# A two-block transformer kernel: modulation moved to VectorE, and norms, ring loads, splits and stores put elsewhere in the program

## The chip, the cores and the metric

The kernel runs on one core of one Trainium2 chip. The metric is the device time of one execution in microseconds (us). Before the change the median of three runs is 3538.93 us, from 3534.08 to 3541.27.

The engines are TensorE (PE, matmuls and weight loads), VectorE (DVE), ScalarE (ACT), GpSimd (POOL) and SyncE (SP, here only a queue that issues DMAs). Each executes its own program in order, and they wait for each other through semaphores.

## What is computed

One sequence of 512 tokens of width 1024 in float32 goes through two blocks.

```python
def first_block(x, ...):
    h = rmsnorm(x, norm_mix_g)
    gq, gk, gv, gr, glr, sq, sk, sv, gate_a, gate_b = split(h @ w_in)
    y_a = gla(gq, gk, gv, log_sigmoid(glr @ w_gk2 + b_gk)) -> rmsnorm * silu(gr) @ w_branch_a
    y_b = sliding window attention(rope(rmsnorm(sq)), rope(rmsnorm(sk)), sv, sinks) @ w_branch_b
    x = x + (sigmoid(gate_a) * y_a + sigmoid(gate_b) * y_b) @ w_out
    return x + peer_layer(rmsnorm(x, norm_ffn_g), ...)

def second_block(x, c, ...):
    shift1, scale1, gate1, shift2, scale2, gate2 = split(silu(c) @ w_ada + b_ada)   # modulation
    h = rms_norm(x, g_mix) * (1 + scale1) + shift1
    q_a, lat, k_r, iq, ik, iw, q_b, k_b, v_b, f_b = split(h @ w_in)
    o_a = attention over the 256 (at most) keys that an indexer (iq, ik, iw) picks, on a latent of rank 128
    o_b = forgetting attention(q_b, k_b, v_b, f_b)
    x = x + gate1 * (concat(rms_norm(o_a, g_out_a), rms_norm(o_b, g_out_b)) @ w_out)
    h2 = rms_norm(x, g_ffn) * (1 + scale2) + shift2
    return rms_norm(x + gate2 * peer_ffn(h2, ...), g_final)
```

`w_ada` is 1024 x 6144, so the modulation is one vector of 1024 times a matrix of 24 MB. A PEER layer scores 128 keys twice for 8 heads, picks 16 of 16,384 experts for each token and head, and computes `sum(gate * gelu(x . u[expert]) * v[expert])`.

## The kernel before, in words

**Precision and ring.** Every product is made of three matmuls in `float32r` (`three`): high by high, high by low, low by high. The weights come in units of 1 MB (128 x 2048). SP loads unit m into a ring of R = 2 slots (L259), ACT rounds it to its high part (`split_hi`, L268), DVE subtracts to get the low part (`split_lo`, L276), and only then may PE use the unit (`unit` waits for it) and SP load unit m + 2 into the slot. The program of each engine is written as a list of calls in the order of the stages; that order alone says what stands ahead of what.

**Stages**, with their times in the profiled execution: the first norm and GLA (0 to 235 us); sliding projections, six units sqkv (235.5 to 349); sliding attention, four blocks n of 128 queries in groups g, with the units ga and wa of branch a between them (349 to 523); the join with units gb, wb, wo (523 to 658); the norm and scores of the first PEER layer (to 773); its up stage, 64 units of `peer_u` in two halves each (to 1402); its down stage, 64 units of `peer_v` (1404 to 1936); the second norm, mixers' projections m2 and qa, keys, dots and qkvb (1936 to 2105); attention turns i = 0 to 17 of the mixers (to 2238); mixed norm and wo2 (to 2320); the second PEER layer, the same way (up from 2320, down from 3006, final norm to 3540).

**Modulation.** SP loads `w_ada` in 30 steps s (10 in the GLA stage, 20 in the sliding stages) into rows of `xres` that are free; POOL multiplies by silu(c) (L548), halves the row twice (L551), and sums into 128 columns (L556, event `ada_sum`); PE sums over partitions with matmuls of one column (L566, `ada_pe`); DVE adds the bias (L577). Some instructions of other stages wait for `ada_sum` too, since they reuse its memory.

**Sliding unit on DVE.** For each unit: sum of squares over a head (L1057), mean and reciprocal (L360, L362), scaling (L1062, L1064), rotation (L350 to L356), a copy to the layout for transposes (L1071), then the split of the unit after next, and the copies of its projection from PSUM (L339).

**PEER.** `peer_order` is a planner that yields `up`, `spread`, `dot` and pick steps in one order, which each engine's program walks. In the spread DVE builds one-hot products (L1791, L1796) that PE multiplies into dense gates; ACT copies them (L1591), SP stores them (`store`, L1419) to `gbuf`; each up unit's gelu is stored to `hbuf` (`keep`, L1411). In the down stage SP fetches both back (`fetch`), DVE and ACT make weighed products Wp (high, low, `weigh_act`, L1852), and PE multiplies them with `peer_v` (L1525). DVE also gathers back single rows (L1758, L1775), loaded by POOL (L1888). At u = 9 of the first down stage DVE makes the second block's row `g_mix * (1 + scale1)` (`modulated_dve`, L1240).

**Mixed norm.** `mixed_act`, `mixed_dve`, `mixed_pe` square all four blocks, take the roots, scale (L2462), transpose all blocks, and only then start wo2.

## Time and profile before

| what | value |
|---|---|
| median of three runs | 3538.93 us (3534.08 to 3541.27) |
| profiled execution, its own time | 3541.71 us |
| its span, first to last instruction | 3539.9 us |
| mean granted clock of TensorE | 0.972 of full speed |
| PE busy | 3338.2 us, 94% |
| DVE busy | 2672.7 us, 76% |
| ACT busy | 1400.4 us, 40% |
| POOL busy | 1031.9 us, 29% |
| DMA, mean over the span | 242 GB/s |

The busy share says that PE has work nearly always; it does not say which wait ends last in a stage. In the timeline each row has the start and length in us, the engine, the line of the kernel and the operation, then what it writes and reads, and in brackets how long the engine was idle before it and which engine's work ended that. A clock of 1.00 is 2.4 GHz and 0.50 is 1.2 GHz; a window that holds both levels has a value between.

### The profile page before, as it was taken

The page shows a single profiled execution, that of the slowest core. Times are in us where ns is not written, and L with a number is a line of the kernel's source. Part 1 is how long each engine was busy: PE and PEld are TensorE (multiplying, and loading weights), DVE is VectorE, ACT ScalarE, POOL GpSimd, SP SyncE. Part 2 cuts the span into 40 slices and gives each one's busy share as a digit, 9 for nine tenths or more (in the row PEclk, how much of TensorE's full clock was granted, in tenths as well). Part 3 has the DMA queues.
Part 4 walks back from the last instruction along what each step waited for, and adds up shares of the span by engine and source line. Part 5 has one row for each costly group of instructions (what it writes and reads, how often), then busy time and mean ns, then how long its engine had stood idle before and what let it go on. Part 6 is the DMA issues. An engine that isn't in the chain of part 4 may idle for free. (4 is left out here: it accounts for less than half of the span.)

```text
span 3539.9 us, 46446 instructions
## 1 busy us (share of the span) xinstructions
PE 3338.2 (94%) x18703; PEld 2946.8 (83%) x18703; DVE 2672.7 (76%) x4561; ACT 1400.4 (40%) x1899; POOL 1031.9 (29%) x652
## 2 busy tenths in 40 slices
PE   8997899999999998999999899889999999999998
PEld 7967558889999898788887786789999898888887
DVE  4458654349999895788888497549999896788888
ACT  4322452233333574233333345333333575333333
POOL 6516700002444330333332000002443331333332
PEclk9998999999999999999999899899999999999999
DMA  6313313237898899899997120226888899999996
GB/s 227 108 51 140 109 54 119 90 99 263 301 326 306 297 345 326 321 359 360 363 360 276 54 72 7 84 73 240 313 314 311 290 349 326 350 362 359 360 361 248
DMA packets 330506, 855.56 MB, mean 242 GB/s; under 512 B 22258, under 2 KB 188066, under 8 KB 297139
## 3 DMA queue, kind: packets, MB, share of 16 engines
q1 hardware_dynamic: 256562, 584.12, 47.1%
q0 software_dynamic: 73728, 268.47, 20.7%
q8 instruction: 147, 2.41, 0.3%
q14 instruction: 69, 0.56, 0.0%
HBM read 746.58 MB, written 105.93 MB: 241 GB/s over the span
## 5 line engine op out<-in xcount | busy, mean ns | idle before, releaser
L293 PE MATMUL ps<-ht_hi,parts 128*128 128x384 f32 (+2 forms) x5088 | 1373.8, 348 | 38.5 <-DVE parts L276 38.1
L276 DVE TENSOR_TENSOR parts<-ring,parts 128x2048 fp32r<-128x2048 f32 (+1 forms) x317 | 741.9, 2340 | 357.0 <-ACT parts L268 356.7
L293 PEld LDWEIGHTS ps<-ht_hi,parts 128*128 128x128 f32 x5088 | 936.6, 191 | 85.7 <-DVE parts L276 48.9
L268 ACT ACTIVATE parts<-ring 128x2048 fp32r<-128x2048 f32 (+1 forms) x317 | 606.7, 1914 | 831.7 <-PE ps L1525 677.2
L293 PE MATMUL ps<-ht_lo,parts 128*128 128x384 f32 (+2 forms) x2544 | 877.5, 345 | 0.0
L1888 POOL DMA_INDIRECT scr<-in_p_rows_u,cst x256 | 403.3, 1575 | 885.9 <-DVE scr L1758 563.9
L335 ACT ACTIVATE scr<-ps 128x384 f32<-128x384 f32 (+2 forms) x497 | 244.4, 505 | 942.0 <-PE ps L293 879.6
L1888 POOL DMA_INDIRECT scr<-in_peer_v,cst x256 | 375.3, 1466 | 770.2 <-DVE xres L1775 620.3
L1525 PE MATMUL ps<-parts,ht_lo 128*128 128x512 f32 x2304 | 530.2, 390 | 6.5 <-DVE ht_lo L1852 6.5
L1525 PE MATMUL ps<-parts,ht_hi 128*128 128x512 f32 x2304 | 529.3, 390 | 4.5 <-DVE ht_hi L1852 4.5
L1525 PEld LDWEIGHTS ps<-parts,ht_lo 128*128 128x128 f32 x2304 | 434.4, 189 | 97.3 <-DVE ht_lo L1852 6.9
L1525 PEld LDWEIGHTS ps<-parts,ht_hi 128*128 128x128 f32 x2304 | 433.5, 188 | 95.3 <-DVE ht_hi L1852 5.1
L293 PEld LDWEIGHTS ps<-ht_lo,parts 128*128 128x128 f32 x2544 | 485.7, 191 | 16.1 <-issue 0.2
L293 PE MATMUL ps<-parts,ht_hi 128*128 128x256 f32 (+1 forms) x1792 | 340.1, 292 | 27.8 <-DVE parts L276 19.9
L1775 DVE SCALAR_TENSOR_TENSOR xres<-scr,cst,xres 128x1024 f32<-128x1024 f32 x255 | 327.5, 1284 | 27.4 <-DVE xres L1775 0.5
L293 PEld LDWEIGHTS ps<-parts,ht_hi 128*128 128x128 f32 x1792 | 292.0, 200 | 29.8 <-DVE parts L276 20.2
L1758 DVE SCALAR_TENSOR_TENSOR scr<-scr,xres 128x1024 f32<-128x1024 f32 x256 | 306.8, 1218 | 4.2 <-DMA scr<-in_p_rows_u,cst 4.0
L293 PE MATMUL ps<-scr 128*128 128x128 f16 (+7 forms) x2272 | 246.6, 272 | 31.6 <-DVE scr L1796 23.2
L293 PE MATMUL ps<-parts,ht_lo 128*128 128x256 f32 (+1 forms) x896 | 260.4, 291 | 0.0
L293 PEld LDWEIGHTS ps<-scr 128*128 128x128 f16 (+3 forms) x2272 | 187.4, 131 | 85.0 <-issue 32.0
L1591 ACT ACTIVATE scr<-ps 128x512 f32<-128x512 f32 x192 | 195.3, 1159 | 24.7 <-PE ps L293 19.7
L339 DVE COPY scr<-ps 128x256 f32<-128x256 f32 (+2 forms) x74 | 37.0, 519 | 196.1 <-PE ps L293 159.1
(255 smaller groups left out, 2787.4 us busy)
## 6 DMA issues: line engine op xcount, KB each, us to landing
ring<-in_peer_u SPq DMA_DIRECT2D x128, 1024.0 KB, 6.8
ring<-in_peer_v SPq DMA_DIRECT2D x128, 1024.0 KB, 7.5
hbuf<-scr SPq DMA_DIRECT2D x128, 384.0 KB, 7.0
gbuf<-scr SPq DMA_DIRECT2D x96, 512.0 KB, 8.6
scr<-gbuf SPq DMA_DIRECT2D x64, 768.0 KB, 9.3
scr<-hbuf SPq DMA_DIRECT2D x64, 768.0 KB, 11.9
ring<-in_w_in SPq DMA_DIRECT2D x35, 1024.0 KB, 5.4
xres<-in_w_ada SPq DMA_DIRECT2D x18, 1024.0 KB, 7.4
```

The costliest lines, as they stand in the source:

```text
L268: e.activation(halves(m)[0], slot_view(m)[:, 0:units[m][0]], ACT.Copy).then_inc(A.sem, A.up(("hi", m)))
L276: e.tensor_tensor(lo, slot_view(m)[:, 0:units[m][0]], hi.bitcast(F32), ALU.subtract).then_inc(V.sem, V.up(("lo", m), ("slot", m)))
L293: ins = e.matmul(ps, l, r, start=(i == 0), stop=(i == n - 1))
L335: e.activation(dst, src, func).then_inc(A.sem, A.up(("free", key), *names))
L339: e.tensor_copy(dst, src).then_inc(V.sem, V.up(("free", key), *names))
L1525: ins = e.matmul(PSt[:, b * 512:(b + 1) * 512], l, r, start=(u == 0 and k == 0), stop=(u == NU - 1 and k == 5), skip_group_check=True)
L1591: e.activation(self.GS[u % 2][:, :, t0:t0 + 4].rearrange("p i t -> p t i"), psum(key).rearrange("p (t i) -> p t i", t=4), ACT.Copy, scale= ...
L1758: e.scalar_tensor_tensor(out=ur, in0=ur, scalar=1.0, in1=X[:, 0, :], op0=ALU.mult, op1=ALU.mult, accum_out=self.HD[:, k:k + 1]).then_inc(V ...
L1775: ins = e.scalar_tensor_tensor(out=x0, in0=vr, scalar=wk, in1=x0, op0=ALU.mult, op1=ALU.add)
L1888: e.indirect_dma_start(rows[k % len(rows)], None, table, bass.IndirectOffsetOnAxis(ap=self.EID[:, k:k + 1], axis=0)).then_inc(s.sem, s.up( ...
```

## The change

- **Modulation.** The POOL programs `ada_pool` and `sliding_pool` are gone. SP loads `w_ada` in 48 steps of 512 KB (128 rows of the contraction by 1024 columns; the host sends it in that layout), 24 in the GLA stage and 24 in the join. DVE multiplies each by its column of silu(c) and adds it to an accumulator of 1024 columns, behind the split of the next unit (`ADA_GLA`, `ADA_JOIN`). PE sums over partitions in 6 groups of 8 matmuls. Nothing of it stands in the sliding stages, and the waits for `ada_sum` there are gone. The split of the unit gr 0 moves between the exponentials; Abs, Exp and Ln of the gate move into gk 0; silu's input c is loaded ahead of the first unit.
- **PEER order.** Two up halves come ahead of spread 0. The last two spread steps come behind the dots, each behind one more up half. A unit's ring load goes ahead of the store of the unit before (`keep`) in the pick phase, and in the tail ahead of the last stores of the gates. The first fetch goes from u = 61 to u = 62. The weighed products of unit 0 have a place of their own (`Wp0`) and don't wait for the last up unit.
- **Second block's row**: `modulated_dve` at u = 20 instead of 9.
- **Mixers.** Positions are the first row loaded; the unit splits stand ahead of the angles; rotation of the index queries and of the keys, and the norm of the latent, stand beside the unit qa; the transposes of qa come behind the dots of block n = 1.
- **Mixed norm** by blocks 3, 2, 1, 0: squares in turns i = 11, 13, 15, 17, and the first wo2 unit takes each block as it is ready.

```diff
+        ADA_GLA = {("gq", 0): (0, 3), ("gq", 1): (3, 6), ("gk", 0): (6, 8), ("gk", 1): (8, 12),
+                   ("gv", 0): (12, 15), ("gv", 1): (15, 18), ("gv", 2): (18, 21), ("gv", 3): (21, 24)}
+        ADA_JOIN = {("gb", 0): (24, 26), ("gb", 1): (26, 30), ("gb", 2): (30, 32), ("gb", 3): (32, 36),
+                    ("wb", 0): (36, 37), ("wb", 1): (37, 38), ("wb", 2): (38, 39), ("wb", 3): (39, 40),
+                    ("wo", 0): (40, 43), ("wo", 1): (43, 46), ("wo", 2): (46, 48)}
...
-        def ada_pool(e, w, s):
-            x = ada_in(s).rearrange("p (h n) -> p h n", n=1024)
-            h = len(ada_cols(s))
-            w.wait_ge(*at_point("c_act"))
-            w.wait_ge(*at_point("ada", s))
-            v = x.rearrange("p h (c n) -> p h c n", c=NC)
-            e.tensor_tensor(v, v, bc(ct.unsqueeze(1).unsqueeze(3), [128, h, NC, 128]), ALU.mult).then_inc(G.sem, G.up())
-            for n in (512, 256):
-                w.wait_ge(*G.now())
...
+            if s >= 24:
+                w.wait_ge(*at_point("pv_pe", NB - 1))
+            if s % 24 >= 4:
+                w.wait_ge(*at_point("ada_used", s - 4))
+            e.dma_start(ada_in(s), inp["w_ada_2"][s]).then_inc(dm_mw[s % 4].sem, dm_mw[s % 4].up(("ada", s), by=16))
...
+        def ada_loads(e, w, span):
+
+            for s in range(span[0] + 4, span[1] + 4):
+                if s // 24 == span[0] // 24:
+                    ada_load(e, w, s)
+
+        def ada_dve(e, w, span):
+            for s in range(*span):
+                cc = s % NC
+                acc = ada_acc(s)
+                w.wait_ge(*at_point("c_act"))
+                w.wait_ge(*at_point("ada", s))
+                if cc == 0:
+                    if s % 24:
+                        ada_sums(e, w, s // NC - 1)
+                    ins = e.tensor_scalar(acc, ada_in(s), ct[:, 0:1], None, ALU.mult)
+                else:
+                    w.wait_ge(*V.now())
+                    ins = e.scalar_tensor_tensor(out=acc, in0=ada_in(s), scalar=ct[:, cc:cc + 1], in1=acc, op0=ALU.mult,
+                                                 op1=ALU.add)
+                ins.then_inc(V.sem, V.up(("ada_used", s)))
...
+        def ada_pe(e, w, k):
+            ps = bank(w, ("mods", k))
+            w.wait_ge(*at_point("ada_used", 8 * k + 7))
+            for j in range(8):
+                ins = e.matmul(ps[:, j:j + 1], ada_acc(8 * k)[:, 128 * j:128 * j + 128], one, start=True, stop=True)
+            ins.then_inc(P.sem, P.up(("ps", ("mods", k))))
...
                     cols_major(e, w, (name, s, 0), v, 0)
+                    if (name, s) == ("gk", 1):
+                        ada_pe(e, w, 0)
                     cols_major(e, w, (name, s, 1), v, 128, ("used", m))
...
-                                                   V.sem, V.up(("free", ("la", blk)), ("la", blk)))
             for s in range(4):
                 split_lo(e, w, U["gv", s] + 1)
+                ada_dve(e, w, ADA_GLA["gv", s])
...
+            split_lo(e, w, U["gr", 0] + 1)
...
@@ -920,7 +900,6 @@
             if part == 2:
                 split_lo(e, w, U["wa", s] + 1)
             if part >= 2:
-                w.wait_ge(*at_point("ada_sum", ADA - 1 if s >= 2 else ADA_HALF - 1))
...
+            for _ in range(2):
+                owed -= pace
+                yield "up", at_u // 2, at_u % 2, False
+                at_u += 1
             for i in range(STEPS):
                 yield "spread", i, 0, 0
                 yield from due(one_step, True)
-            yield "spread", STEPS, 0, 0
-            yield "spread", STEPS + 1, 0, 0
             while slot < SLOTS:
                 yield "dot", slot, 0, 0
                 slot += 1
+            for i in range(2):
+                yield "up", at_u // 2, at_u % 2, False
+                at_u += 1
+                yield "spread", STEPS + i, 0, 0
...
+                self.Wp0 = parts_at(2048, 4 * ND).rearrange("p (s j t) -> p s j t", s=2, j=2)
...
+            def W(self, u):
+
+                return self.Wp[u % 4] if u else self.Wp0
...
                 for kind, a, b, _ in order:
                     if kind == "up":
+                        if a not in late and b == 0:
+                            load(e, w, U[tag + "u", a] + R + 1)
                         if b == 0 and a:
                             self.keep(e, w, a - 1)
-                        if b == (1 if a in late else 0):
+                        if a in late and b == 1:
                             load(e, w, U[tag + "u", a] + R + 1)
-                        if (a, b) == (NU - 3, 0):
+                        if (a, b) == (NU - 2, 0):
                             self.fetch(e, w, 0)
                     if kind == "spread" and a >= 4 and a % 4 < 2:
...
             def weigh_act(self, e, w, u):
                 g = u // 2
-                w.wait_ge(*(self.pt("down", u - 4) if u >= 4 else at_point("used", U[self.tag + "u", NU - 1])))
+                if u:
...
-                    if u == 9 and self.nq == 16:
+                    if u == 20 and self.nq == 16:
                         modulated_dve(e, w, "n2", 4096, 6144)
 
...
+            sp_small(e, "positions", POS, inp["positions_2"])
+            sp_row(e, "latent_gain", gkv, row("g_kv_2"))
             sp_row(e, "forget_bias", fb, row("b_forget_2"))
-            sp_row(e, "latent_gain", gkv, row("g_kv_2"))
-            sp_small(e, "positions", POS, inp["positions_2"])
...
-                transposes(e, w, ("iqt", blk), [M2[:, blk, 144 + j * 128:144 + (j + 1) * 128] for j in range(2)])
+                if (name, s) == ("qa", 0):
+                    w.wait_ge(*at_point("iq_turned"))
+                    for blk in range(NB):
+                        transposes(e, w, ("iqt", blk), [M2[:, blk, 144 + j * 128:144 + (j + 1) * 128] for j in range(2)])
+                    w.wait_ge(*at_point("latent"))
...
+                if n == 1:
+                    w.wait_ge(*at_point("qa_turned"))
+                    for blk in range(NB):
+                        transposes(e, w, ("qat", blk), [QA[:, blk, j * 128:(j + 1) * 128] for j in range(4)])
             for s in range(4):
...
+                    w.wait_ge(*at_point("angles"))
+                    e.activation(SIN, RR.rearrange("p (b j) -> p b j", b=NB), ACT.Sin)
+                    e.activation(COS, RC.rearrange("p (b j) -> p b j", b=NB), ACT.Sin).then_inc(A.sem, A.up(("cos2",)))
+                if (name, s) == ("qa", 0):
+                    latent_squares(e, w)
...
                     ins.then_inc(A.sem, A.up(("exp2", i)))
+                if i in (11, 13, 15, 17):
+                    mixed_squares(e, w, 3 - (i - 11) // 2)
+                if i == 16:
+                    for blk in (3, 2, 1):
+                        mixed_root(e, w, blk)
...
+
+        def mixers_dve(e, w):
+            for (name, s), n, dst in m2_parts:
+                split_lo(e, w, U[name, s] + 1)
+                if (name, s) == ("qa", 0):
+                    turned_keys(e, w)
+                for blk in (1, 3):
+                    put_dve(e, w, (name, s, blk), dst[:, blk, :], psum((name, s, blk))[:, 0:n], (name, "dve"))
+                if (name, s) == ("m2", 0):
+                    angles_dve(e, w)
+                if (name, s) == ("qa", 0):
+                    for blk in (1, 3):
+                        put_dve(e, w, ("iqt", blk), IQT[:, :, blk * 128:(blk + 1) * 128],
+                                psum(("iqt", blk))[:, 0:256].rearrange("p (k t) -> p k t", k=2), ("iqt", 1))
...
+        def mixed_turn(e, w, blk):
+            w.wait_ge(*at_point("mix_normed", blk))
+            for j0 in (0, 4):
+                transposes(e, w, ("mt", blk, j0), [MIX[:, blk, j * 128:(j + 1) * 128] for j in range(j0, j0 + 4)])
+
...
-                for j0 in (0, 4):
-                    transposes(e, w, ("mt", blk, j0), [MIX[:, blk, j * 128:(j + 1) * 128] for j in range(j0, j0 + 4)])
-            w.wait_ge(*at_point("ht", "mix"))
-            for s in range(4):
+            for blk in (3, 2, 1):
+                mixed_turn(e, w, blk)
+            m = U["wo2", 0]
+            v = unit(w, m)
+            for blk in (3, 2, 1, 0):
+                w.wait_ge(*at_point("ht", "mix", blk))
+                rows_major(e, w, ("wo2", 0, blk), v, 256, blk, *([("used", m)] if blk == 0 else []))
+                if blk == 3:
+                    mixed_turn(e, w, 0)
+            for s in (1, 2, 3):
                 m = U["wo2", s]
...
-                    e.scalar_tensor_tensor(out=mv, in0=mv, scalar=ssm[:, 2 * blk + s:2 * blk + s + 1],
-                                           in1=go[:, 512 * s:512 * s + 512], op0=ALU.mult, op1=ALU.mult).then_inc(
-                                               V.sem, V.up(("mix_normed", blk)))
-                if blk:
-                    mixed_low(e, w, blk - 1)
-            mixed_low(e, w, NB - 1)
+            for blk in (3, 2, 1):
+                mixed_mean(e, w, blk)
+            for blk in (3, 2, 1):
+                mixed_row(e, w, blk)
+            mixed_low(e, w, 3)
+            mixed_mean(e, w, 0)
+            mixed_row(e, w, 0)
+            for blk in (2, 1, 0):
+                mixed_low(e, w, blk)
```

Three places show how instructions move.

The first is VectorE's order in the GLA stage, from the split made while unit gk 1 is in use on to the first units gv. Before:

```order
L276 TENSOR_TENSOR parts<-ring,parts 128x2048
L339 COPY scr<-ps 128x512
L276 TENSOR_TENSOR parts<-ring,parts 128x2048
L339 COPY scr<-ps 128x256 x2
L276 TENSOR_TENSOR parts<-ring,parts 128x2048
L339 COPY scr<-ps 128x256 x2
```

Now:

```order
L276 TENSOR_TENSOR parts<-ring,parts 128x2048
L557 TENSOR_TENSOR mod_t<-ps,mod_t 128x8
L545 TENSOR_SCALAR scr<-xres,scr 128x1024
L548 SCALAR_TENSOR_TENSOR scr<-xres,scr 128x1024 x3
L339 COPY scr<-ps 128x512
L276 TENSOR_TENSOR parts<-ring,parts 128x2048
L548 SCALAR_TENSOR_TENSOR scr<-xres,scr 128x1024 x3
L339 COPY scr<-ps 128x256 x2
L276 TENSOR_TENSOR parts<-ring,parts 128x2048
L548 SCALAR_TENSOR_TENSOR scr<-xres,scr 128x1024
L557 TENSOR_TENSOR mod_t<-ps,mod_t 128x8
```

L548 and L545 are the products; each run of them stands behind a split (L276) and ahead of the copies from PSUM (L339), and L557 adds the bias to a group of columns.

The second is SP's queue at the end of the first up stage (`in_peer_u` is an up unit, `in_peer_v` a down unit, a store goes to `gbuf` or `hbuf`, a fetch comes from them). Before:

```order
L1419 DMA gbuf<-scr 128x8x128 x2
L1411 DMA hbuf<-scr 128x768 [waits act_done]
L1419 DMA gbuf<-scr 128x8x128 [waits act_done]
L1419 DMA gbuf<-scr 128x8x128 x3
L259 DMA ring<-in_peer_u 128x2048 [waits dve_done]
L1411 DMA hbuf<-scr 128x768 [waits act_done]
L259 DMA ring<-in_peer_v 128x2048 [waits dve_done]
L1431 DMA scr<-gbuf 128x1536 [waits g_stored1,g_stored0]
```

Now:

```order
L259 DMA ring<-in_peer_u 128x2048 [waits dve_done]
L1420 DMA gbuf<-scr 128x8x128 [waits act_done]
L1420 DMA gbuf<-scr 128x8x128
L259 DMA ring<-in_peer_v 128x2048 [waits dve_done]
L1412 DMA hbuf<-scr 128x768 [waits act_done]
L1420 DMA gbuf<-scr 128x8x128 x2
L259 DMA ring<-in_peer_v 128x2048 [waits dve_done]
L1412 DMA hbuf<-scr 128x768 [waits act_done]
L1432 DMA scr<-gbuf 128x1536 [waits g_stored1,g_stored0]
L1439 DMA scr<-hbuf 128x1536 [waits h_kept1,h_kept0]
```

The last load of an up unit stood behind four stores to `gbuf` and now stands ahead of them, and the first down unit's load stands between the stores; the first fetch stands behind one more load.

The third is VectorE's order from the last attention turn to the first wo2 split (L360 and L362 before, L2505 and L2510 now, are mean and reciprocal; L2462 and L2515 scale a block's half; L347 makes the low part of a transposed block). Before:

```order
L360 TENSOR_SCALAR scr<-scr 128x8
L362 RECIPROCAL scr<-scr 128x8
L2462 SCALAR_TENSOR_TENSOR scr<-scr 128x512 x4
L347 TENSOR_TENSOR ht_lo<-ps,ht_hi 128x4x128 x2
L2462 SCALAR_TENSOR_TENSOR scr<-scr 128x512 x2
L347 TENSOR_TENSOR ht_lo<-ps,ht_hi 128x4x128 x2
L2462 SCALAR_TENSOR_TENSOR scr<-scr 128x512 x2
L347 TENSOR_TENSOR ht_lo<-ps,ht_hi 128x4x128 x4
L1240 SCALAR_TENSOR_TENSOR scr<-scr 128x1024
```

Now:

```order
L2505 TENSOR_SCALAR scr<-scr 128x2 x3
L2510 RECIPROCAL scr<-scr 128x2
L2515 SCALAR_TENSOR_TENSOR scr<-scr 128x512 x2
L2510 RECIPROCAL scr<-scr 128x2
L2515 SCALAR_TENSOR_TENSOR scr<-scr 128x512 x2
L2510 RECIPROCAL scr<-scr 128x2
L2515 SCALAR_TENSOR_TENSOR scr<-scr 128x512 x2
L347 TENSOR_TENSOR ht_lo<-ps,ht_hi 128x4x128 x2
L2505 TENSOR_SCALAR scr<-scr 128x2
L2510 RECIPROCAL scr<-scr 128x2
L2515 SCALAR_TENSOR_TENSOR scr<-scr 128x512 x2
L347 TENSOR_TENSOR ht_lo<-ps,ht_hi 128x4x128 x6
```

Means and reciprocals are taken by block, and block 0's stand behind the low part of block 3.

## Rows read from the trace of the kernel before

**Rows 1.** Windows by stage: start:end, length, busy of each engine, clock, DMA share and rate.

```profile
0.00:235.55 235.55, 217.75 (x1328) 180.87 (x1328) 97.03 (x97) 83.90 (x135) 102.45 (x47) 0.97 0.39 130
235.55:349.26 113.71, 89.71 (x681) 88.55 (x681) 103.12 (x117) 29.62 (x46) 69.46 (x28) 0.88 0.35 122
349.26:522.80 173.54, 154.90 (x705) 99.89 (x705) 96.79 (x164) 84.22 (x209) 69.00 (x52) 0.94 0.28 91
522.80:658.00 135.20, 132.24 (x745) 116.69 (x744) 55.78 (x58) 40.82 (x39) 0.00 (x0) 0.99 0.35 111
1165.00:1364.60 199.60, 189.36 (x1561) 182.06 (x1562) 192.56 (x185) 138.49 (x144) 56.63 (x31) 0.97 0.98 324
```

**Rows 2.** Timeline of VectorE and GpSimd, one unit's norm and rotation: start, length, instruction.

```profile
254.03 1.22 DVE L1057 TENSOR_REDUCE scr<-scr 128x16 f32<-128x1024 f32 x1
...
272.68 5.69 DVE L276 TENSOR_TENSOR parts<-ring,parts 128x2048 fp32r<-128x2048 f32 x1
...
286.29 3.76 POOL L548 TENSOR_TENSOR xres<-xres,scr 128x2048 f32<-128x2048 f32 x1 [3.52 <-DMA xres<-in_w_ada]
...
286.61 3.99 DVE L1071 COPY scr<-scr 128x1024 f32<-128x1024 f32 x1
...
296.84 1.22 DVE L1057 TENSOR_REDUCE scr<-scr 128x16 f32<-128x1024 f32 x1 [1.19 <-ACT scr L1047]
...
302.83 0.69 DVE L1071 COPY scr<-scr 128x1024 f32<-128x1024 f32 x1
```

**Rows 3.** Timeline of TensorE behind waits, GLA to the attention loop: [idle before <-releaser].

```profile
140.56 0.58 PE L566 MATMUL ps<-cst,scr 128*128 128x1 f32 x2 [6.40 <-POOL scr L556]
...
278.42 0.58 PE L293 MATMUL ps<-parts,ht_hi 128*128 128x256 f32 x1 [13.71 <-DVE parts L276]
...
427.68 0.48 PE L329 MATMUL ps<-cst,scr 128*128 128x128 f32 x1 [5.61 <-DVE scr L1126]
...
475.65 0.33 PE L329 MATMUL ps<-cst,scr 128*128 128x128 f32 x1 [1.45 <-DVE scr L1126]
```

**Rows 4.** The page's groups of instructions and DMA issues, whole span.

```profile
L276 DVE TENSOR_TENSOR parts<-ring,parts 128x2048 fp32r<-128x2048 f32 (+1 forms) x317 | 741.9, 2340 | 357.0 <-ACT parts L268 356.7
...
L1775 DVE SCALAR_TENSOR_TENSOR xres<-scr,cst,xres 128x1024 f32<-128x1024 f32 x255 | 327.5, 1284 | 27.4 <-DVE xres L1775 0.5
...
xres<-in_w_ada SPq DMA_DIRECT2D x18, 1024.0 KB, 7.4
```

**Rows 5.** Timeline of TensorE, start of the first spread.

```profile
1167.57 1.89 PE L293 MATMUL ps<-scr 128*128 128x128 f16 x16 [4.13 <-DVE scr L1796]
```

**Rows 6.** Tail of the up stages: SyncE's queue, TensorE's waits, DMA, one window.

```profile
1367.28 10.35 SPq L1419 DMA_DIRECT2D gbuf<-scr  x4
...
1391.56 0.69 PE L293 MATMUL ps<-ht_hi,parts 128*128 128x384 f32 x1 [6.10 <-DVE parts L276]
...
1404.44 0.50 PE L1525 MATMUL ps<-parts,ht_hi 128*128 128x512 f32 x1 [2.25 <-DVE ht_hi L1852]
...
2993.89 0.69 PE L293 MATMUL ps<-ht_hi,parts 128*128 128x384 f32 x1 [4.58 <-DVE parts L276]
...
DMA packets 6150, 11.57 MB, mean 331 GB/s; under 512 B 280, under 2 KB 4376, under 8 KB 5648
...
1385.00:1400.00 15.00, 8.90 (x40) 8.58 (x39) 5.61 (x4) 5.07 (x5) 0.00 (x0) 0.77 0.99 392
```

**Rows 7.** Timeline in the first down stage, VectorE and TensorE.

```profile
1487.47 1.23 DVE L1240 SCALAR_TENSOR_TENSOR scr<-scr 128x1024 f32<-128x1024 f32 x1 [9.42 <-DMA scr<-in_g_mix]
...
1492.83 0.80 PE L1525 MATMUL ps<-parts,ht_lo 128*128 128x512 f32 x1 [6.51 <-DVE ht_lo L1852]
```

**Rows 8.** Head of the mixers: TensorE's waits.

```profile
1965.79 0.53 PE L293 MATMUL ps<-parts,ht_hi 128*128 128x192 f32 x1 [6.21 <-DVE parts L276]
...
2008.94 0.48 PE L329 MATMUL ps<-cst,scr 128*128 128x128 f32 x1 [5.82 <-DVE scr L356]
```

**Rows 9.** Window of the mixed norm, columns as in rows 1.

```profile
2232.00:2263.00 31.00, 16.83 (x71) 14.86 (x72) 15.22 (x22) 16.97 (x39) 0.00 (x0) 0.50 0.36 136
```

320 lines of the change are left out of this document (142 added, 178 removed).

## The prediction

> **What bounds the kernel now.** I read the stage windows first [rows 1]: how long each stage is, how much of it TensorE (PE) was busy, and the clock it was granted. PE fills 94% of the span, so a gain is a stall of PE removed, the half clock (1.2 instead of 2.4 GHz) behind it, or fewer PE instructions. In a window the clock loses length x (1 - PEclk). Then I listed PE's waits over 0.5 us with the engine that ended each, and followed each back on that engine. They lie in three kinds of place: where GpSimd (POOL) computes the modulation (24.0 us idle of 113.7 in the sliding projections and 18.6 of 173.5 in the attention loop [rows 1]), at the ends and heads of stages [rows 5 to 9], and around the spread. Most of the rest, the long down stages above all, is PE without stalls, and no edit touches it.
>
> **1. Modulation from POOL to VectorE (DVE).** While POOL multiplies, DVE stretches. In [rows 2] the norm-and-rotate chain of one unit, from L1057 to the split behind L1071, takes 272.68 - 254.03 = 18.7 us beside POOL; in a place where POOL is idle the same chain takes 302.83 + 0.69 - 296.84 = 6.7. The copy L1071, begun 0.3 us after POOL's L548 of 3.76 us, takes 3.99 against 0.69. POOL is busy without a break beside the slow chain. The split at its end takes 5.69, where the mean of all splits is 2.34 [rows 4]. PE waited 13.71 us for that split [rows 3].
> The Trainium skill, page "SBUF — State Buffer", section "Who interferes with whom", calls the port that the two engines share an exclusive lock, and says that a DVE instruction with two SBUF inputs contends with a GpSimd instruction that reads SBUF. This would speak against moving the products to DVE only if POOL kept reading SBUF beside them; by that rule the two GLA memsets that stay on POOL cost nothing, and if they did contend it would be once their own length. The copy of 3.99 fits a lock, which ends with POOL's instruction, better than a shared bandwidth.
> What DVE gets: 48 products of 128x1024. The nearest row is L1775 of the same form, 1284 ns [rows 4]; with its semaphore I take 1.33, so 64 us, 32 in the GLA stage and 32 in the join, none in the sliding stages. DVE is busy 97.0 of 235.6 us and 55.8 of 135.2 there [rows 1], so on the mean it fits. Unit by unit: a unit gets at most four products, 5.3 us, beside a split of 2.34 and its copies from PSUM (four of 128x256 at most, under 2 us by L1071's 0.69 for four times the columns): 7 to 9.5 us, and a unit of PE is longer, 13.3 in the sliding stage by the sum below. They stand behind the split of the next unit (first order piece), so PE's weights go first, and what waits behind the products is only the copies that free PSUM. With that cover gone a unit would be late by its products, 4.0 to 5.3.
> - GLA: the stall of 6.40 for POOL's L556 [rows 3] goes but for about 0.8 (the split of gr 0 now stands among the exponentials). Of the stage's clock loss, 0.03 x 235.6 = 7, I take the 2.4 behind this stall. Gain 8.
> - Sliding projections: of 24.0 idle, 1.5 is a wait for the GLA output and 1.0 stays by my count, so 21.5. The clock costs 0.12 x 113.7 = 13.6, about half of it while PE was idle anyway; I take 7.5. With the chain at 6.7, DVE needs about 6.7 + 2.3 + 1.5 for copies = 10.5 us per unit, against (89.7 - 7.5 - 2.6 of modulation matmuls) / 6 = 13.3 of PE: late next is the chain again, with 2.8 us to spare. Gain 29.
> - Attention loop: the gap of 5.61 becomes its quiet twin of 1.45 [rows 3]; the other turns likewise. Of 18.6 idle I take 8.9, of 0.06 x 173.5 = 10.4 of clock 6.1. Gain 15.
> - The 48 columns of 128x1 matmuls come in 6 groups instead of 30. The first two of a group took 0.58 [rows 3]; 24 starts fewer at 0.2 is 5 (bounds 0, and 24 x 0.58 = 14).
> Sum 57. Lower bound 20: only the waits of 6.40 and 13.71 go. Upper 75: nearly all idle and clock of the two sliding stages.
>
> **2. Spread.** Two `up` halves go before spread 0. PE waits 4.13 [rows 5] and some shorter times for the first one-hot products. But DVE is busy 192.56 of 199.60 us [rows 1]: the spread ends when DVE ends, and the split pulled ahead merely moves. Bounds 0 (or a little lost, as the split delays the first one-hots by 2.29) to 4 each; I take 3, for two layers 6.
>
> **3. Tail of the up stage.** Four stores hold SP's queue 10.35 us; only then is the last ring load issued, and PE waits 6.10, in the second layer 4.58 [rows 6]. Now the load goes first (second order piece). The stall goes and most of the clock: the window is at 0.77 over 15 us, 3.4, of which I take 2. The first unit's weighed products also go to a place of their own, so that they don't wait for the last `up`; this aims at the gap of 2.25 before the first down product. I don't count on it: they need a fetch of h whose store stands behind the stores now, and if it lands no earlier than it did, the gap grows by what the ups gain. Gains 7 and 6, together 13; bounds 3 (only the order of the same bytes changes) and 18.
> DMA moves 331 GB/s over 35 us (11.57 MB) and 392 over the last 15 of them, at a share of 0.99 [rows 6]. The Trainium skill, "HBM Reference" and the section "Bandwidth" of "DMA: Bandwidth & Descriptors", gives about 358 GB/s per core when two cores share, and about 425 for one that streams alone. By 358 the 11.57 MB need 32.3 us and the tail can give back 2.7; by 425 they need 27.2, 7.8 to gain. The row of 392 goes against 358 as a limit here.
>
> **4. Second norm's rows.** DVE waited 9.42 us for the row g_mix at u = 9, and PE behind it 6.51 [rows 7]. At u = 20 the row has long landed and the cover is the down stage's DVE slack. 6.51 and 2.7 of clock (the tail's window had 3.4 for a like stall): 9.2. Bounds 5 and 10.
>
> **5. Head of the mixers.** PE waits 6.21 for a split that stands behind the angles, and those behind positions [rows 8]. With splits first the 6.2 go, and of the clock behind a stall of this length I take 3.0 (again the tail's 3.4): 9.2. Then the keys' rotation and the latent norm move beside the qa unit and the qa transposes behind the dots of n = 1: the gap of 5.82 [rows 8] and two smaller ones of 2.3 in all go (PE stands 8.1 of these 31.4 us), 8.1, and 0.4 of clock. Late next are the index keys copied into four rows: the gap of 5.82 ends with rotations that still stand ahead of them, but they now start a unit earlier. 17.7; bounds 7 and 20.
>
> **6. Mixed norm by blocks.** 31 us hold 16.83 of PE, all at half clock [rows 9]. Squares of three blocks now run in the last attention turns, and the first wo2 unit starts block by block (third order piece). Idle 14.2 becomes about 5 (block 0 ends with the last turn: square, root, row, transposes), clock 8.4 becomes 2.1: 15.5. Bounds 7 and 20.
>
> **Rest.** c goes before the first weight load: +0.45 us of issue on the path. Exp and Ln of the gate in gk 0, and the load before keep in the pick phase: no PE wait there names them; nothing.
> Sum 57 + 6 + 13 + 9.2 + 17.7 + 15.5 - 0.45 = 118. The profiled execution took 3541.7 us, 2.8 above the median of the runs, so 3423.7 on its scale and 3421 on the median's; I say **3422**.
>
> **Rivals.**
> - **The stretch is only partly POOL's**, or the products take DVE's slack so that PSUM is freed late. For it: the chain's 12 us of stretch are spread over many short instructions, and 2.8 us of slack per sliding unit is thin. Against: the copy of 3.99 starts and ends with a POOL instruction. Part 1 gives its lower bound 20: 3422 + 37 = **3459**, chance 0.15.
> - **New waits in the norms.** Parts 5 and 6 put DVE chains ahead of PSUM copies and ACT squares into turns that ACT fills. For it: DVE in order, eight short steps in a row. Against: beside them stand whole units of PE. Parts 5 and 6 give 8 instead of 33: **3447**, chance 0.12.
> - **The tail is bound by bytes**: DMA's share is 0.99 [rows 6], so each byte put ahead puts another behind. Against: the last ring load waits for SP's queue, not for bytes. Part 3 gives 2 instead of 13: **3433**, chance 0.10. That the edit does nothing there is the same case.
> - **Slower: SP blocked by the products.** Each load of w_ada waits for DVE to have used a buffer, and the next ring load stands behind it in SP's queue. If each of the 19 units that carry products gets its weights late by a landing of 7.4 us (w_ada's load [rows 4]), that is 141 us against 118: **3562**, 22 above 3540; it decides from 118 / 19 = 6.2 us per unit. Against: the load of unit m waits for DVE's split anyway, which stands ahead of these products. Chance 0.03.
> The forecast keeps the other 0.60. Low end: parts 1 and 6 a third better, 3396. High end 3472: the first rival with a little of the second. Within 0.2% (7 us, about what a measurement of this kernel can tell from no change) lies 0.01, where the last rival stops halfway; slower 0.03, faster 0.96.
>
> **What would show it.** L1071 at 0.69 us in every sliding unit, chain 6.7; PE idle under 4 us in the sliding projections, whose length would be near 82 us against 113.7; no POOL busy before 658; PE gap before the last up unit gone; the first wo2 matmul some 14 us sooner after the last turn; mixers' keys without the gap of 5.82; total PE busy down by some 35 us with clock 0.98 to 0.99. Wrong if the sliding chain stays above 9 us, if PE waits for DVE in gv or gb units, or if the gap before down grows past 6 us.

## The result, and the profile after

The changed kernel took 3444.45 us in the median of four runs (3440.23 to 3448.08), against 3536.51 us for the kernel before on the same chip: ratio 0.9741, 95% interval 0.972 to 0.9761. The forecast was 3422 with a range of 3396 to 3472: right in direction, and within the range, but 22 us too low. The gain was 92 us by the medians and 96.1 by the two profiled spans (3539.9 and 3443.8), where 118 were forecast. TensorE's busy time fell by 26.9 us (3338.2 to 3311.3), where the prediction named some 35, and its mean granted clock rose from 0.972 to 0.985, as it said.

From the page of the changed kernel, busy time by engine:

```profile
PE 3311.3 (96%) x18703; PEld 2918.5 (85%) x18703; DVE 2667.5 (77%) x4619; ACT 1394.7 (40%) x1902; POOL 794.3 (23%) x532
```

Windows by stage of the changed kernel (GLA, sliding projections, sliding attention, first spread, a stretch of the first down stage), columns as in [rows 1]. The border between the first two stands at another matmul than in [rows 1]: at the one that ran at 240.80 here and at 248.79 before, 13 us into the projections.

```profile
0.00:240.80 240.80, 227.59 (x1433) 190.78 (x1433) 125.90 (x147) 87.60 (x140) 3.42 (x7) 1.00 0.41 137
240.80:308.56 67.76, 66.75 (x561) 66.31 (x561) 56.17 (x94) 25.20 (x40) 0.00 (x0) 1.00 0.28 88
308.56:468.10 159.54, 149.27 (x674) 94.12 (x675) 81.15 (x164) 84.46 (x209) 0.00 (x0) 0.97 0.18 56
1125.00:1324.00 199.00, 187.02 (x1536) 179.64 (x1534) 186.27 (x181) 138.71 (x144) 60.01 (x36) 0.97 0.98 322
1434.00:1600.00 166.00, 166.00 (x734) 137.43 (x734) 139.73 (x146) 57.80 (x63) 66.98 (x44) 1.00 0.97 371
```

The sliding projections from that same matmul in the kernel before, and the changed kernel's from the matmul at which [rows 1] begins them:

```profile
248.79:349.26 100.47, 77.94 (x584) 76.99 (x585) 91.18 (x94) 25.43 (x40) 69.46 (x28) 0.86 0.39 138
```

```profile
227.57:308.56 80.99, 78.53 (x658) 77.89 (x657) 68.11 (x117) 29.38 (x46) 0.00 (x0) 1.00 0.24 75
```

So the stage is 81.0 us long where it was 113.7, near the 82 of the forecast, and TensorE stands 2.5 us in it instead of 24.0. Beside [rows 2], VectorE in the same chain of the changed kernel:

```profile
246.04 1.22 DVE L1031 TENSOR_REDUCE scr<-scr 128x16 f32<-128x1024 f32 x1
247.30 0.17 DVE L360 TENSOR_SCALAR scr<-scr 128x16 f32<-128x16 f32 x1
...
249.30 1.22 DVE L1038 TENSOR_TENSOR scr<-scr 128x1024 f32<-128x1024 f32 x1
...
252.02 0.69 DVE L1045 COPY scr<-scr 128x1024 f32<-128x1024 f32 x1
252.63 2.29 DVE L276 TENSOR_TENSOR parts<-ring,parts 128x2048 fp32r<-128x2048 f32 x1
```

The chain is 6.6 us (246.04 to 252.63) where [rows 2] had 18.7, and the copy 0.69 where one of [rows 2], in the next unit, had 3.99.

To see where the time went I matched TensorE's groups of matmuls of the two traces one by one and took the distance between their starts at the border of each stage. It grows where a stage gained (a negative number is a loss):

| part | forecast, us | measured, us |
|---|---|---|
| 1 modulation, all | 57 | 51.7: GLA 8.0, sliding projections 32.7, attention loop 14.5, join -3.5 |
| pick phases of both layers | 0 | -5.2, of which 1.2 is clock |
| 2 spread, both layers | 6 | -0.8 |
| 3 tail of the ups, both layers | 13 | 7.4 (3.7 each) |
| 4 second block's row | 9.2 | 9.4 |
| 5 head of the mixers | 17.7 | 17.6 |
| 6 mixed norm | 15.5 | 15.9 |
| sum | 118 | 96.0 |

Parts 4, 5 and 6 came out within 0.4 us. So did the sliding projections: 29 were forecast for waits and clock, and their small matmuls, 3.3 us of busy time, left besides.

The head of the mixers, before and now, and then the mixed norm, before and now, each between the same two matmuls (columns as in [rows 1]; what TensorE is not busy, it stands):

```profile
1936.21:2105.16 168.95, 148.58 (x901) 131.79 (x899) 115.37 (x253) 68.80 (x115) 4.14 (x6) 0.92 0.25 82
```

```profile
1874.25:2025.57 151.32, 141.70 (x902) 124.86 (x900) 115.40 (x253) 68.31 (x115) 4.14 (x6) 0.98 0.29 91
```

```profile
2232.00:2263.85 31.85, 17.68 (x78) 15.71 (x79) 15.25 (x23) 16.97 (x39) 0.00 (x0) 0.52 0.36 134
```

```profile
2153.20:2168.80 15.60, 12.06 (x78) 11.27 (x79) 10.78 (x24) 11.31 (x32) 0.00 (x0) 0.78 0.58 236
```

What is left of the waits of [rows 5, 6] in the changed kernel, and what is new, in time order:

```profile
1005.33 0.87 ACT L335 ACTIVATE scr<-ps 128x384 f32<-128x384 f32 x2 [3.49 <-DMA hbuf<-scr]
1006.04 0.44 PE L293 MATMUL ps<-ht_hi,parts 128*128 128x384 f32 x1 [1.04 <-DVE parts L276]
1016.65 0.49 ACT L335 ACTIVATE scr<-ps 128x384 f32<-128x384 f32 x1 [8.65 <-DMA hbuf<-scr]
...
1127.84 1.07 PE L293 MATMUL ps<-scr 128*128 128x128 f16 x16 [2.47 <-DVE scr L1798]
1131.38 1.89 PE L293 MATMUL ps<-scr 128*128 128x128 f16 x16 [2.48 <-DVE scr L1798]
...
1327.30 5.08 SPq L1420 DMA_DIRECT2D gbuf<-scr  x2
1332.97 2.88 SPq L259 DMA_DIRECT2D ring<-in_peer_v  x1
1335.90 0.43 SPq L1412 DMA_DIRECT2D hbuf<-scr  x1
1339.01 0.32 SPq L1432 DMA_DIRECT2D scr<-gbuf  x1
1339.43 0.38 SPq L1439 DMA_DIRECT2D scr<-hbuf  x1
...
1347.12 0.56 DVE L1846 TENSOR_TENSOR scr<-scr 128x384 f32<-128x384 f32 x1 [5.85 <-DMA scr<-hbuf]
1349.35 0.79 PE L1526 MATMUL ps<-parts,scr_parts 128*128 128x512 f32 x1 [4.42 <-DVE scr_parts L1854]
```

In the pick phase ScalarE, which never waited for `hbuf` there before, waits for it in most units, 81 times in the whole trace. Ahead of the spread the one stall of 4.13 [rows 5] has become several shorter ones, 2.47 and 2.48 the longest. In the tail the wait of 6.10 is gone, but the one before the first down product grew from 2.25 [rows 6] to 4.42, and the first down unit took 10.96 us instead of 8.44, at half clock in part.

### The profile page after: what moved, and what is told of

It is laid out like the page before. It is cut to its first block and busy times, and to the rows that moved or that the text cites. A ratio compares the mean times of both kernels' runs of the same rounds, so it can differ in the third digit from the quotient of the medians.

```text
span 3443.8 us, 46427 instructions
## 1 busy us (share of the span) xinstructions
PE 3311.3 (96%) x18703; PEld 2918.5 (85%) x18703; DVE 2667.5 (77%) x4619; ACT 1394.7 (40%) x1902; POOL 794.3 (23%) x532
## 5 line engine op out<-in xcount | busy, mean ns | idle before, releaser
L276 DVE TENSOR_TENSOR parts<-ring,parts 128x2048 fp32r<-128x2048 f32 (+1 forms) x317 | 724.1, 2284 | 340.3 <-ACT parts L268 339.9
L1526 PE MATMUL ps<-parts,ht_hi 128*128 128x512 f32 x2232 | 511.1, 389 | 0.0
L293 PEld LDWEIGHTS ps<-ht_lo,parts 128*128 128x128 f32 x2544 | 484.1, 190 | 15.9 <-issue 0.2
L1526 PEld LDWEIGHTS ps<-parts,ht_hi 128*128 128x128 f32 x2232 | 419.0, 188 | 87.0
L293 PE MATMUL ps<-parts,ht_hi 128*128 128x256 f32 (+1 forms) x1792 | 326.3, 285 | 2.7 <-DVE ht_lo L1199 1.2
L293 PEld LDWEIGHTS ps<-parts,ht_hi 128*128 128x128 f32 x1792 | 281.0, 193 | 4.1 <-DVE ht_lo L347 1.7
```

What stands on the lines that cost most here:

```text
L276: e.tensor_tensor(lo, slot_view(m)[:, 0:units[m][0]], hi.bitcast(F32), ALU.subtract).then_inc(V.sem, V.up(("lo", m), ("slot", m)))
L293: ins = e.matmul(ps, l, r, start=(i == 0), stop=(i == n - 1))
L1526: ins = e.matmul(PSt[:, b * 512:(b + 1) * 512], l, r, start=(u == 0 and k == 0), stop=(u == NU - 1 and k == 5), skip_group_check=True)
```

## The experiments

Each ran beside the kernel before on one chip; the ratio is to that kernel, and 0.9741 (0.972 to 0.9761) is the changed kernel's.

**b1_pool_left_out**, the kernel before without GpSimd's product and halvings, so that its modulation is not computed:

```diff
-            v = x.rearrange("p h (c n) -> p h c n", c=NC)
-            e.tensor_tensor(v, v, bc(ct.unsqueeze(1).unsqueeze(3), [128, h, NC, 128]), ALU.mult).then_inc(G.sem, G.up())
-            for n in (512, 256):
-                w.wait_ge(*G.now())
-                e.tensor_tensor(x[:, :, 0:n], x[:, :, 0:n], x[:, :, n:2 * n], ALU.add).then_inc(G.sem, G.up())
-            w.wait_ge(*G.now())
```

> The kernel before, but GpSimd leaves out the modulation's product and the two halvings of each row (its loads, the last small sum and the matmuls stay, so the modulation is not computed). Theory (the stretch of VectorE is GpSimd's reading of SBUF): what the change gained in GLA, sliding projections and attention loop by its own trace, 8.0 + 32.7 + 14.5 us, comes here too but for the small matmul groups (about 8): 3536 - 47 = 3489 us, the copy behind the rotation at 0.69 us in every unit, sliding projections 84 us instead of 113.7. Rival (the stretch is not GpSimd's; the change gained by taking waits away): only the waits that named GpSimd go, some 10 us, 3526, and the copy still takes 3 to 4 us beside the loads.

3492.07 us, ratio 0.9877 (0.986 to 0.9893). Its sliding projections:

```profile
245.49:315.88 70.39, 69.38 (x584) 68.94 (x585) 58.23 (x94) 25.20 (x40) 6.33 (x7) 1.00 0.56 190
```

From the same matmul it was 100.5 us before (248.79 to 349.26). So 30.1 of the 32.7 come from GpSimd's silence alone, though all loads stayed; of GLA 3.3, of the loop 12.3. The theory holds.

**p1_pool_reads** and **p2_pool_writes**, the changed kernel with work for GpSimd whose results nobody needs, from the end of GLA. VectorE waits for its end only in the attention loop. p1:

```diff
+            for i in range(8):
+                w.wait_ge(*G.now())
+                e.tensor_tensor(v, v, bc(ct.unsqueeze(1).unsqueeze(3), [128, 2, NC, 128]), ALU.mult).then_inc(G.sem, G.up())
+                for n in (512, 256):
+                    w.wait_ge(*G.now())
+                    e.tensor_tensor(x[:, :, 0:n], x[:, :, 0:n], x[:, :, n:2 * n], ALU.add).then_inc(G.sem, G.up(("filler",)))
```

p2:

```diff
+            for i in range(38):
+                w.wait_ge(*G.now())
+                e.memset(Xt[:, 0:2048], 0.0).then_inc(G.sem, G.up(("filler",)))
```

> The changed kernel, with eight rounds of GpSimd's old work (product of 128x2048, halvings to 1024 and 512) on rows of xres that nothing reads, from the start of the sliding projections on; no other engine waits for it there. Theory: some 70 us of GpSimd bring the stretch back, the norm-and-rotate chain 12 to 18 us instead of 6.7, sliding projections 67.8 to about 97 us, 3444 + 30 = 3474. Rival (the old stalls were waits for modulation results or its loads, not contention): 3444, chain 6.7.

> The same place and about the same 70 us of GpSimd, but memsets of 128x2048 that only write. Theory that only an instruction reading SBUF on GpSimd holds up a VectorE instruction with two SBUF inputs: products, splits and rotations keep their length, only the plain copy may wait for the end of one memset (1.8 us): sliding projections 68 to 72 us, 3444 to 3449. Rival (any work of GpSimd stretches VectorE): as with the reading work, 90 us or more, 3470.

p1: 3487.01 us, 0.9855 (0.9838 to 0.9871). p2: 3452.43, 0.9757 (0.9741 to 0.9774). The sliding projections, p1 and then p2:

```profile
243.15:349.89 106.74, 75.04 (x560) 73.52 (x561) 96.18 (x94) 25.31 (x40) 70.70 (x24) 0.82 0.18 56
```

```profile
240.54:315.97 75.43, 70.10 (x561) 68.42 (x561) 66.79 (x94) 25.64 (x40) 71.77 (x38) 0.95 0.27 83
```

GpSimd is busy 71 us in both; with reads the stage takes 39.0 us more than the changed kernel's 67.8 (TensorE stands 30.7 us longer, the rest is clock), with writes 7.7. GpSimd, VectorE and TensorE in p1:

```profile
252.69 4.48 POOL L2707 TENSOR_TENSOR xres<-xres,scr 128x2048 f32<-128x2048 f32 x1
```

```profile
253.73 4.52 DVE L1039 TENSOR_TENSOR scr<-scr 128x1024 f32<-128x1024 f32 x1
...
272.16 0.58 PE L293 MATMUL ps<-parts,ht_hi 128*128 128x256 f32 x1 [13.44 <-DVE parts L276]
```

and VectorE in p2, under an unbroken row of memsets:

```profile
247.04 1.00 DVE L360 TENSOR_SCALAR scr<-scr 128x16 f32<-128x16 f32 x1
...
249.87 1.23 DVE L1039 TENSOR_TENSOR scr<-scr 128x1024 f32<-128x1024 f32 x1
...
252.59 1.56 DVE L1046 COPY scr<-scr 128x1024 f32<-128x1024 f32 x1
254.08 2.27 DVE L276 TENSOR_TENSOR parts<-ring,parts 128x2048 fp32r<-128x2048 f32 x1
```

The scaling of 1.22 us, begun 1.0 us after a reading product of 4.48, took 4.52 and ended 1.1 us after it: blocked, not shared. Under memsets the scaling and the split keep their 1.23 and 2.27, and only the copy (0.69 to 1.56) and the small tensor_scalar (0.17 to 1.00) wait. The Trainium skill, "SBUF — State Buffer", section "Who interferes with whom", says that an instruction with two SBUF inputs contends with GpSimd's reads and not with its writes, and that `copy` and `tensor_scalar` can enter modes that take both ports and so contend with GpSimd. Both traces agree. I had expected at most 72 us for p2's stage; it is 75.4, since the copies' waits also made TensorE stand 3.6 us before the last unit's transposes.

**d_products_twice**, each of the 42 accumulating products made twice, so that the modulation comes out wrong:

```diff
-                    w.wait_ge(*V.now())
-                    ins = e.scalar_tensor_tensor(out=acc, in0=ada_in(s), scalar=ct[:, cc:cc + 1], in1=acc, op0=ALU.mult,
-                                                 op1=ALU.add)
+                    for _ in range(2):
+                        w.wait_ge(*V.now())
+                        ins = e.scalar_tensor_tensor(out=acc, in0=ada_in(s), scalar=ct[:, cc:cc + 1], in1=acc, op0=ALU.mult,
+                                                     op1=ALU.add)
+                        if not _:
+                            ins.then_inc(V.sem, V.up())
```

> The changed kernel with each of the 42 accumulating products of the modulation executed twice (the modulation is then wrong), 42 x 1.33 = 56 us more on VectorE, 28 in GLA and 28 in the join. Theory (the products lie under TensorE's units): 0 to 8 us more, 3444 to 3452, mostly where VectorE has 8 products in a unit. Rival (no cover left): 30 us or more, 3474 to 3500.

3468.78 us, 0.9808 (0.9791 to 0.9824): 24 us more, between the two. By the matched groups GLA lost 14.7 and the join 7.5 of 28 each. GLA's loss stands here:

```profile
96.75 0.59 PE L567 MATMUL ps<-cst,scr 128*128 128x1 f32 x2 [2.79 <-DVE scr L549]
...
131.58 0.58 PE L567 MATMUL ps<-cst,scr 128*128 128x1 f32 x2 [3.88 <-DVE scr L549]
```

TensorE waits for the last product of a group of eight. The two waits are 6.7 of the 14.7; nearly all the rest is half clock behind them. The products that the change added, 58.4 us of VectorE in its trace, are hidden, but not far from the edge: I had summed a unit's products against a unit of TensorE and not asked when the group's sum is due.

**gr0_back**, the split of the second gr unit behind the exponentials again, on VectorE (shown) and on ScalarE:

```diff
-            split_lo(e, w, U["gr", 0] + 1)
...
-            for s in range(1, 4):
+            for s in range(4):
                 split_lo(e, w, U["gr", s] + 1)
```

> The changed kernel with the split of the second gr unit behind the exponentials and products of GLA again, in its old place. Theory (of the 8.0 us that the GLA stage gained, GpSimd's absence gave the 3.3 that came when its products were left out of the kernel before, and this move the other 4.7): TensorE waits about 4.2 us for that split after the first gr unit, as it did there, GLA ends 4 to 5 us later, 3444 + 4.5 = 3449. Rival (without GpSimd the exponentials' chain is short enough and the move gives nothing): 3444, no wait there.

3452.45 us, 0.9755 (0.9739 to 0.9772). The wait is there:

```profile
148.58 0.80 PE L293 MATMUL ps<-parts,ht_hi 128*128 128x256 f32 x2 [4.93 <-DVE parts L276]
```

By the matched groups the kernel loses 5.9 us at this wait, and 2.4 more to half clock ahead of it, at places that the edit doesn't touch. So the move of one split gives the larger part of the 8.0 that GLA gained, and GpSimd's absence some 2 to 3 (b1 had 3.3). In the forecast both stood in one line.

The 8.0 is partly luck. Ten traces here run the same program up to this border (the changed kernel, its repeat, p1, p2, s_no_pull, w_no_wp0, u9, k_keep_first, best3, best2), and they gained 4.3 to 8.6 us on the kernel before; half clock took nothing from the fastest three, the changed kernel among them, and 5.1 us from the slowest.

**s_no_pull**, without the two up halves ahead of the spread:

```diff
-            for _ in range(2):
-                owed -= pace
-                yield "up", at_u // 2, at_u % 2, False
-                at_u += 1
```

> The changed kernel without the two up halves ahead of the first spread step (they come where the planner puts them, the last stores stay moved). Theory (VectorE sets the length of the spread, so TensorE's wait for the first one-hot products only moves): the spread and the ups end within 1 us of where they ended, 3444, with a wait of about 4 us before the first one-hot product again. Rival (the pulled ups hide that wait): 3 to 4 us later per layer, 3451.

3445.43 us, 0.9733 (0.9714 to 0.9753). The totals don't tell them apart; the matched groups do. From the last pick to the last up, this kernel is 2.4 us shorter than the changed one in the first layer and 0.3 in the second, although TensorE stands 4.13 us ahead of its first one-hot product again. Of the 2.4, up to 1.7 is clock: it took 5.1 us from the first spread of the changed kernel and 3.4 here, and 5.1 from the second spread of both. The pulled halves give nothing and cost a little: in nine traces with them the first spread takes 203.1 to 204.0 us, in the five without (this one, the kernel before, b1, best3, best2) 201.2 to 203.3.

**w_no_wp0**:

```diff
-                return self.Wp[u % 4] if u else self.Wp0
+                return self.Wp[u % 4]
...
-                if u:
+                if True:
                     w.wait_ge(*(self.pt("down", u - 4) if u >= 4 else at_point("used", U[self.tag + "u", NU - 1])))
```

> The changed kernel with unit 0's weighed products back in their old place, waiting for the last up unit. Theory (the fetch of h, which lands 2.2 us after the last up half has ended, comes last, so the own place buys nothing): the wait before the first down product 4.4 us as now, 3444. Rival (the own place works): 2 us later per layer, 3448.

3446.88 us, 0.9737 (0.9718 to 0.9757), and

```profile
1351.39 0.79 PE L1525 MATMUL ps<-parts,ht_hi 128*128 128x512 f32 x1 [4.14 <-DVE ht_hi L1853]
```

against 4.42: the place of its own is worth nothing while the fetch comes last.

**u9**:

```diff
-                    if u == 20 and self.nq == 16:
+                    if u == 9 and self.nq == 16:
```

> The changed kernel with the second block's row made at u = 9 again. Theory: VectorE waits again for the row g_mix, TensorE stands 6.5 us and runs 2.7 us longer at half clock, 3444 + 9 = 3453. Rival (the row lands sooner in the new tail): no wait, 3444.

3451.07 us, 0.9749 (0.973 to 0.9769):

```profile
1441.18 0.79 PE L1526 MATMUL ps<-parts,ht_lo 128*128 128x512 f32 x1 [6.86 <-DVE ht_lo L1854]
```

The wait of [rows 7] is back, and its unit takes 11.35 us instead of 8.32.

**k_keep_first**, the store of gelu ahead of the ring load in the pick phase:

```diff
-                        if a not in late and b == 0:
+                        if a not in late and a >= NU - 4 and b == 0:
                             load(e, w, U[tag + "u", a] + R + 1)
                         if b == 0 and a:
                             self.keep(e, w, a - 1)
+                        if a < NU - 4 and a not in late and b == 0:
+                            load(e, w, U[tag + "u", a] + R + 1)
```

> The changed kernel, where in the pick phase the store of the gelu output is again issued ahead of the ring load (the tail keeps the new order). Theory (the load waits for a split some 4 us later, so the store behind it lands late, ScalarE waits for it and the split behind ScalarE is late): the waits near units 32 to 36 in each layer go, 2.4 and 1.2 us sooner, ScalarE no longer waits for hbuf: 3440. Rival (those small waits come from the picks' order): 3444.

3439.97 us, 0.9722 (0.9706 to 0.9739). The intervals overlap; the trace decides. Between units 24 and 40 it gains 2.6 us in the first layer and 1.45 in the second, ScalarE waits for `hbuf` 4 times instead of 81, and in the unit where the changed kernel waited it waits for TensorE again:

```profile
1006.46 0.49 ACT L335 ACTIVATE scr<-ps 128x384 f32<-128x384 f32 x1 [3.61 <-PE ps L293]
```

The direction holds beyond this pair of traces, the size less so. Against the kernel before, units 24 to 40 of the first layer lose 0.5 to 3.4 us in the nine traces of these kernels with the load first. In the three with the store first they gain 0.1 (here), gain 0.1 (best2) and lose 1.6 (best3, which has one more stretch of half clock there).

**after_again, best3, best2**, all three on one chip. after_again is the changed kernel unaltered. best3 is k_keep_first and s_no_pull in one, with the fetch of h for the first down units issued one unit earlier; best2 also issues the gates' fetch ahead of the next ring load. best2, of which best3 lacks the first piece:

```diff
+                        if (a, b) == (NU - 2, 0):
+                            self.fetch(e, w, 0)
+                            load(e, w, U[tag + "u", a] + R + 1)
...
+                        if (a, b) == (NU - 3, 0):
+                            self.fetch_h(e, w, 0)
...
+                if g:
+                    self.fetch_h(e, w, g)
+
+            def fetch_h(self, e, w, g):
```

> The changed kernel unaltered, as the measure for the two below on the same chip: 3444 us.

> The changed kernel with three edits: gelu stores ahead of ring loads in the pick phase, no up halves pulled ahead of the spread, and the fetch of h for the first two down units issued one unit earlier, apart from that of the gates. Theory: 4.0 + 2.7 us from the first two (what their single runs showed in the traces) and 1.5 us per layer from the third, since the gates' fetch alone then comes last: 3444 - 9.7 = 3434.5, wait before the first down product about 3 us. Rival (the third does nothing, the gates' fetch lands as late as h did): 3437.5, wait above 4.

> As the last, and the gates' fetch also issued ahead of the second down unit's ring load. Theory (1 MB less ahead of it in the DMA queues): the fetch lands up to 2 us sooner, wait before the first down product about 1 us, 3444 - 13 = 3431. Rival (the queue SP is held by the wait for the last gate stores, and the ring load behind it comes late): a new wait before the second down unit, 3436 or more.

3446.32 us, 0.9748 (0.9734 to 0.9763); 3439.75, 0.9721 (0.9708 to 0.9735); 3433.97, 0.9709 (0.9696 to 0.9722). VectorE and TensorE at the start of the down stage, best3 and then best2:

```profile
1347.36 1.03 DVE L1850 TENSOR_TENSOR scr<-scr 128x384 f32<-128x384 f32 x2 [5.71 <-DMA scr<-gbuf]
...
1349.59 0.80 PE L1530 MATMUL ps<-parts,scr_parts 128*128 128x512 f32 x1 [4.27 <-DVE scr_parts L1858]
```

```profile
1336.30 0.33 SPq L1433 DMA_DIRECT2D scr<-gbuf  x1
...
1340.52 0.56 DVE L1851 TENSOR_TENSOR scr<-scr 128x384 f32<-128x384 f32 x1 [3.37 <-DMA scr<-gbuf]
1343.06 0.61 PE L1531 MATMUL ps<-parts,scr_parts 128*128 128x512 f32 x1 [2.25 <-DVE scr_parts L1859]
```

In best3 the theory of the early fetch fell: the gates' fetch lands as late as h did, and the wait stays (4.27, 5.29 in the second layer). In best2 the fetch, with one load of 1 MB fewer ahead of it, lands 4.2 us after its issue instead of some 6, the wait is 2.25 in both layers, and no wait appears before the second down unit. By the matched groups both tails together give 12.7 us in best2, where the changed kernel got 7.4. best2 is faster than the changed kernel by 12.3 us of median, with intervals apart: the fastest here.

## Why the prediction was right or wrong

**Modulation.** Mechanism and size held: 51.7 against 57. GpSimd's reads stretch VectorE (p1 against p2), and the first rival, a stretch only partly GpSimd's, is out (b1). The prediction read the copy of [rows 2] as ending with GpSimd's product; by its rows it ended 0.55 us after it (286.61 + 3.99 against 286.29 + 3.76), which a copy of 0.69 us blocked until then fits as well.

Two terms were mis-sized. The small matmul groups were to give 5 us: their busy time in the three stages was 13.1 us (5.40, 3.31 and 4.42) and is 11.3 now (5.7 in GLA, 5.5 in the join), so they gave 1.9. That is also why the join lost 3.5: three groups run there now and none did. And the attention loop, forecast at 15, gave 14.5 with its groups in it, whose busy time of up to 4.4 went too, so 10 to 12 for the rest. Its idle time came out as forecast (159.5 - 149.3 = 10.3 us, with 18.6 - 8.9 = 9.7 expected). Its busy time fell by 5.6 (154.9 to 149.3), where 6.1 were taken for the clock alone. The window still loses 0.03 x 159.5 = 4.8 us to the clock: waits of 1.45 and 0.7 us, the same in each turn, were followed by half clock in one turn of the changed kernel and not in another. The third and the fourth turn:

```profile
419.12 1.94 PE L329 MATMUL ps<-cst,scr 128*128 128x128 f32 x8 [0.46 <-DVE scr L1098]
421.74 5.82 PE L969 MATMUL ps<-scr 128*64 128x256 f32 x32 [0.69 <-ACT scr L335]
...
462.05 1.09 PE L329 MATMUL ps<-cst,scr 128*128 128x128 f32 x8 [0.45 <-DVE scr L1098]
463.87 3.73 PE L969 MATMUL ps<-scr 128*64 128x256 f32 x32 [0.74 <-ACT scr L335]
```

**"Exp and Ln of the gate in gk 0, and the load before keep in the pick phase: no PE wait there names them; nothing."** This is the step that failed outright: -4.0 us without the clock. No wait before the change named the store because the store was on time. The load waits for a split some 4 us later, the store of gelu behind it in SP's queue lands later, ScalarE waits to reuse that buffer, and its part of the split is late for TensorE (k_keep_first). The prediction says of the tail that each byte put ahead puts another behind; the pick phase needed the same question.

**Spread.** I wrote that the spread ends when VectorE ends, and yet took 3 us a layer. The argument was right and the number did not follow it: measured -0.8 in all, and s_no_pull gives the cost of the pulled halves, 2.4 and 0.3 with the clock in them.

**Tail.** 7.4 against 13. The ring load ahead of the stores did what was said: the ups ended 8.4 and 6.2 us sooner. I named the fetch as what is late next, "the gap grows by what the ups gain", but priced only the old 2.25 as staying. It grew by 2.2 and 1.5, and the half clock behind it cost the first down unit another 2.5 and 1.0. The rival of a tail bound by bytes is half right: not the last ring load but the fetch was held by what stood ahead of it (best2). With that fetch moved the tails gave 12.7, so the forecast 13 was there to gain, in an order that the changed kernel doesn't have. The lower of the two DMA rates that the prediction weighs would have left 2.7 us in a tail; it is not the limit here, as 407 GB/s in the last window of this document shows.

**Second block's row, head, mixed norm.** Right within 0.4 us; u9 shows the first alone. For the other two I rely on the matched traces: no experiment undid them. In the head the sum hides two errors that cancel, which is luck: the waits of 6.21 and 5.82 are gone, but the others grew a little, so TensorE's idle time fell by 10.8 us (20.4 to 9.6) where 14.3 were forecast, and its busy time, by the clock, by 6.9 where 3.4 were. In the mixed norm idle time fell by 10.6 (9.2 forecast) and busy time by 5.6 (6.3).

**The slower rival**, SP blocked by the products, did not happen; d_products_twice shows that with 28 us more in GLA TensorE waits at the group sums, not for weights.

## What to carry to other kernels

A wait of TensorE that disappears is worth its length and the half clock behind it, less what the next late thing in that place takes back; price that next thing with a number before summing. When an issue is moved ahead of another in a DMA queue, follow the one that is now behind, also where no wait of the old trace names it. GpSimd's elementwise work that reads SBUF is not free beside VectorE: here 71 us of it made a stage 39 us longer.

## What the runs showed of the hardware

A GpSimd memset of 128x2048 beside VectorE left an instruction with two SBUF inputs at 1.23 us but took a copy from 0.69 to 1.56. SP's issue of two stores took 5.08 us in the tail, at 1327 us. From 1340 us on, a single core's DMA moved 407 GB/s:

```profile
1340.00:1361.00 21.00, 16.58 (x69) 13.94 (x68) 8.52 (x12) 5.39 (x9) 0.00 (x0) 0.84 1.00 407
```

And TensorE's clock made two profiled executions of one program (the changed kernel and after_again) differ by 1 to 3 us at the same places, which is why effects of that size were read from matched groups between two nearby matmuls and not from totals.
